# Expert feed-forward of a fused kernel: tokens fetched by indirect transfers, 18 weight slots, 12 of them loaded in the last projection

## The reference, cut to what matters

```
def expert_choice_ffn(xn, router_w, w_gate, w_up, w_down):
    b, n, d = xn.shape
    cap = CAPACITY_FACTOR * n // N_EXPERTS          # 64
    logits = jnp.einsum('bnd,de->ben', xn, router_w).astype(jnp.float32)
    aff = jax.nn.softmax(logits, axis=1)            # over the experts
    gate, idx = lax.top_k(aff, cap)
    xg = jax.vmap(lambda xs, ix: xs[ix])(xn, idx)
    hid = jax.nn.silu(jnp.einsum('becd,edf->becf', xg, w_gate)) * jnp.einsum('becd,edf->becf', xg, w_up)
    y = jnp.einsum('becf,efd->becd', hid, w_down) * gate[..., None].astype(xn.dtype)
    scatter = lambda ix, ys: jnp.zeros((n, d), ys.dtype).at[ix.reshape(-1)].add(ys.reshape(-1, d))
    return jax.vmap(scatter)(idx, y)
```

## Time and profile before

| | us |
|---|---|
| median of 3 executions | 3516.3 |
| lowest and highest | 3516.07, 3517.92 |
| span of the profiled execution | 3517.1 |
| TensorE busy in the span | 3333.0 (95%) |
| VectorE busy | 1738.0 |
| ScalarE busy | 673.3 |
| GpSimd busy | 302.6 |
| transfers: bytes, mean rate | 453.36 MB, 129 GB/s |
| expert part | from about 2972 to the end |

### The profile page before, as it was taken

The page is one execution under the profiler, slowest core; times in us unless marked ns, Lnnn a source line. Parts: engine busy times, 40 slices in busy tenths (PEclk is TensorE's granted clock), DMA queues, the critical chain, the costliest instruction groups (busy, mean ns, idle before and its releaser), DMA issues. The chain is left out here.

```text
span 3517.1 us, 39734 instructions
## 1 busy us (share of the span) xinstructions
PE 3333.0 (95%) x15231; PEld 2389.2 (68%) x15231; DVE 1738.0 (49%) x2533; ACT 673.3 (19%) x1097; POOL 302.6 (9%) x238
## 2 busy tenths in 40 slices
PE   6999998999999999999899999899989998899998
PEld 5888854488887888855478887555765887434342
DVE  4665457366646666348276644524336655211122
ACT  1111015111101111013221100531553101100001
POOL 2111000111100111000101100100330000000000
PEclk9999998999999999999899999999999999999999
DMA  5443221334322433222224321322113232899996
GB/s 134 117 104 102 80 60 36 84 90 117 95 82 84 115 94 101 91 56 60 70 74 114 94 90 48 92 72 84 43 30 90 84 108 100 355 409 409 410 410 267
DMA packets 469520, 453.36 MB, mean 129 GB/s; under 512 B 33867, under 2 KB 418174, under 8 KB 469149
## 3 DMA queue, kind: packets, MB, share of 16 engines
q1 hardware_dynamic: 467312, 449.97, 39.8%
q10 hardware_dynamic: 1452, 1.67, 0.4%
q0 software_dynamic: 640, 0.15, 0.0%
HBM read 445.96 MB, written 5.77 MB: 128 GB/s over the span
## 5 line engine op out<-in xcount | busy, mean ns | idle before, releaser
L465 PE MATMUL psum<-arena 128*128 128x256 f32 x7392 | 1616.2, 380 | 2.3 <-DVE arena L814 2.3
L465 PEld LDWEIGHTS psum<-arena 128*128 128x128 f32 x7392 | 1398.9, 190 | 203.9 <-issue 7.0
L879 DVE TENSOR_TENSOR arena<-arena 128x512 f32<-128x512 f32 (+2 forms) x152 | 96.4, 634 | 602.7 <-PE psum L465 573.6
L2360 PE MATMUL psum<-arena 128*64 128x512 f32 x1536 | 345.8, 600 | 1.6 <-ACT arena L2457 1.6
L354 POOL TENSOR_TENSOR arena<-arena 128x1024 f32<-128x1024 f32 x96 | 180.9, 1906 | 1037.6 <-DVE arena L869 993.0
L2360 PEld LDWEIGHTS psum<-arena 128*64 128x64 f32 x1536 | 104.8, 137 | 235.5 <-issue 228.4
L703 ACT COPY arena<-psum 128x256 f32<-128x256 f32 x104 | 38.9, 374 | 1177.1 <-PE psum L465 1177.0
L1677 PE MATMUL psum<-arena 128*128 128x256 f32 x1120 | 243.0, 379 | 1.4 <-DVE arena L2082 1.4
L1677 PEld LDWEIGHTS psum<-arena 128*128 128x128 f32 x1120 | 211.7, 189 | 32.6 <-DVE arena L2082 1.8
L575 PE MATMUL psum<-arena 128*128 128x512 f32 x416 | 183.1, 595 | 10.0 <-DVE arena L1021 6.3
L869 DVE TENSOR_REDUCE arena<-arena 128x256 f32<-128x2048 f32 x48 | 177.5, 3698 | 0.0
(11 more groups left out here) (422 smaller groups left out, 3011.9 us busy)
## 6 DMA issues: line engine op xcount, KB each, us to landing
arena<-in_w_gate_dram SPq DMA_DIRECT2D x64, 1024.0 KB, 14.0
arena<-in_w_up_dram SPq DMA_DIRECT2D x64, 1024.0 KB, 15.0
arena<-in_w_down_dram SPq DMA_DIRECT2D x64, 1024.0 KB, 17.4
arena<-in_ffn_w_gate_dram SPq DMA_DIRECT2D x88, 512.0 KB, 6.2
arena<-in_ffn_w_up_dram SPq DMA_DIRECT2D x88, 512.0 KB, 7.2
arena<-in_ffn_w_down_dram SPq DMA_DIRECT2D x96, 384.0 KB, 3.7
arena<-in_w_in_dram SPq DMA_DIRECT2D x144, 256.0 KB, 3.2
arena<-in_ada_w_dram SPq DMA_DIRECT2D x48, 512.0 KB, 4.0
```

The lines of the kernel that those rows point to most:

```text
L465: mm = pe.matmul(psum[:, b0 + b, c:c + HT], w, right(x), start=(first and c == 0), stop=last, skip_group_check=True)
L879: dve.tensor_tensor(sv[:, 0, :, :], a21, a22, ALU.add)
L2360: mm = pe.matmul(psum[64 * e:64 * e + 64, bank0 + half, :], x[:, k, 64 * e:64 * e + 64], ring[u % SLOTS][:, e, half * 512:(half + 1) * 512 ...
```

## The change

Weights: 18 slots instead of 12. Twelve of them lie in places of `arena` that the last projection no longer uses; their loads (0 to 11, the gate weights of pair 0 and four of up) are issued in the mixer, four each behind `joint_load` 16, 17 and 18. Six more follow in the head: 12 and 13 once the squares are used, 16 and 17 once the residual is transposed, 14 and 15 once the token rows are written out. Tokens: the normalised rows `xf_tok` are written to device memory (2 MB). For each pair, the two row matmuls (`rows_of`) now come first, VectorE computes for each of the 128 places its token's number (`tokens_of`), and GpSimd fetches the 128 rows of 4 KB by one indirect transfer; PE transposes them in eight matmuls (`gathered`) instead of multiplying with `one_hot`. Within a pair `put_back` lies after units 3, 5, 7 and 9, two before and two after the transposes; `rows_of(q + 1)` after unit 11, `gathered(q + 1)` after the fifth down unit. All loops are written out. The final norm's weight is loaded after the last expert load.

```diff
@@ second_mixer_program
+        dead = ((xm_at, xm_at + 2048), (xm_at + 24576, xm_at + 26624), (xm_at + 4096, xm_at + 6144),
+                (xm_at + 20480, xm_at + 22528), (xm_at + 12288, xm_at + 14336), (xm_at + 28672, xm_at + 30720))
+        mem["slots_from"] = xm_at
+        mem["expert_slots"] = [arena[:, at:at + 2048].rearrange("p (e c) -> p e c", e=2) for two in dead for at in two]
...
+            early = mem["expert_slots"]
             for u in range(16, 20):
                 joint_load(u, "w_o_2", (u - 16) * 256)
+                if u < 19:
+                    sp.wait_ge(unit_done, JOINT + u)
+                    for n in range(4 * (u - 16), 4 * (u - 16) + 4):
+                        name, k = ("w_gate_2", "w_up_2")[n // KT], n % KT
+                        src = d[name][0, 0:2, k * 128:(k + 1) * 128, :]
+                        sp.dma_start(early[n], src.rearrange("e p c -> p e c")).then_inc(mem["expert_in"][n], 16)
@@ experts_program, SyncE
+            sp.wait_ge(s["var_done"], 1)
+            load(12)
+            load(13)
+            sp.wait_ge(s["tok_ok"], 2 * NT)
+            load(16)
+            load(17)
+            for t in range(NT):
+                sp.wait_ge(s["xf_ok"], t + 1)
+                sp.dma_start(xf_dram[t * 128:(t + 1) * 128, :], xf_tok[:, t, :]).then_inc(s["xf_out"], 16)
+            sp.wait_ge(s["xf_out"], 16 * NT)
+            load(14)
+            load(15)
+            for n in range(SLOTS, UNITS * PAIRS):
+                sp.wait_ge(s["unit_used"], used(n - SLOTS))
+                load(n)
+            last = UNITS * PAIRS - SLOTS + (2 - UNITS * PAIRS) % SLOTS
+            sp.wait_ge(s["unit_used"], used(last))
+            sp.dma_start(final_w, d["final_norm_w_2"].partition_broadcast(128)).then_inc(s["final_in"], 16)
@@ GpSimd
+            pool.wait_ge(s["xf_out"], 16 * NT)
+            for q in range(PAIRS):
+                pool.wait_ge(s["token_ok"], q + 1)
+                if q:
+                    pool.wait_ge(s["xg_tr"], 2 * q)
+                pool.indirect_dma_start(xg_tok, None, xf_dram,
+                                        bass.IndirectOffsetOnAxis(ap=index[:, 0:1], axis=0))\
+                    .then_inc(s["gather_in"], 16)
@@ TensorE
+            def gathered(q):
+                pe.wait_ge(s["gather_in"], 16 * q + 16)
                 for k in range(KT):
-                    for t in range(NT):
-                        mm = pe.matmul(psum[:, 4 + k // 4, (k % 4) * 128:(k % 4 + 1) * 128],
-                                       xf_tok[:, t, k * 128:(k + 1) * 128],
-                                       one_hot[:, t, bass.ds(q * 128, 128)],
-                                       start=(t == 0), stop=(t == NT - 1))
+                    mm = pe.transpose(psum[:, 2 + k // 4, (k % 4) * 128:(k % 4 + 1) * 128],
+                                      xg_tok[:, k * 128:(k + 1) * 128], ident)
+                    if k % 4 == 3:
+                        mm.then_inc(s["xg_tr"], 1)
...
             for u in range(2 * KT):
+                    both_experts(2 * (u // KT), xg, UNITS * q + u, u % KT)
+                    if q and u in (3, 5, 7, 9):
+                        put_back_after(q - 1, (u - 3) // 2)
+                    if u == 11 and q + 1 < PAIRS:
+                        pe.wait_ge(s["silu_ok"], q + 1)
+                        rows_of(q + 1)
+                if q:
+                    for m in (4, 5):
+                        put_back_after(q - 1, m)
...
+                    both_experts(6, hidT, UNITS * q + 2 * KT + k, k)
+                    if k == 4 and q + 1 < PAIRS:
+                        gathered(q + 1)
@@ VectorE
+            dve.tensor_tensor_scan(token_iota, xg_tok[:, 0:T], xg_tok[:, 0:T], 0.0, ALU.mult, ALU.add)
...
+            def tokens_of(q):
+
+                sc = scatters[:, q % 3, :]
+                dve.wait_ge(s["rows_done"], q + 1)
+                dve.tensor_scalar(sc, psum[:, 0, :], slot_of_part, None, ALU.is_equal)
+                dve.drain()
+                dve.scalar_tensor_tensor(out=xg_tok[:, 0:T], in0=token_iota, scalar=1.0, in1=sc,
+                                         op0=ALU.mult, op1=ALU.mult, accum_out=token)
+                dve.drain()
+                dve.tensor_scalar(index[:, 0:1], token, -1.0, None, ALU.add)
+                dve.scalar_tensor_tensor(out=xg_tok[:, T:2 * T], in0=psum[:, 1, :], scalar=1.0, in1=sc,
+                                         op0=ALU.mult, op1=ALU.mult, accum_out=gates[:, q % 2:q % 2 + 1])
```

More of the change, by code:

```diff
@@ L2378, in pair @@
                 for u in range(2 * KT):
[L2379 to L2392, removed]
@@ L2403, in pair @@
[L2403 to L2408, removed]
-            pe.wait_ge(s["hot_ok"], 1)
-            pe.wait_ge(s["tok_ok"], 2 * NT + 2)
-            pe.wait_ge(s["xf_ok"], NT)
-            gather(0)
-            pair(0, 1, 1)
-            with pe.Fori(0, PAIRS - 2) as i:
-                pair(i + 1, 0, 1)
@@ L2417, in _ @@
-            pair(PAIRS - 1, 0, 0)
+                    if k % 4 == 3:
+                        mm.then_inc(s["hT_done"], 1)
+                if q:
+                    for m in (6, 7):
+                        put_back_after(q - 1, m)
+                for k in range(KT):
+                    if k == 0:
+                        pe.wait_ge(s["hT_act"], q + 1)
+                    if k == 4:
+                        pe.wait_ge(s["hT_dve"], q + 1)
+                    both_experts(6, hidT, UNITS * q + 2 * KT + k, k)
+                    if k == 4 and q + 1 < PAIRS:
+                        gathered(q + 1)
@@ L2418, in _ @@
+            pe.wait_ge(s["slot_ok"], 1)
+            pe.wait_ge(s["const_in"], 32)
+            rows_of(0)
+            gathered(0)
+            for q in range(PAIRS):
+                pair(q)
             for m in range(2 * NT):
                 if m >= 4:
-                    pe.wait_ge(s["res_ok"], KT * (PAIRS - 1) + m - 3)
+                    pe.wait_ge(s["res_ok"], 8 * (PAIRS - 1) + m - 3)
                 put_back(PAIRS - 1, m, m % 4)
@@ L2575, in _ @@
-            gathered()
             def add_back(q, m, bank):
@@ L2583, in weigh @@
             def weigh(q):
-                dve.wait_ge(s["unit_used"], q * 24 + (SLOTS + 3 * KT))
-                dve.scalar_tensor_tensor(out=y, in0=psum[:, 6:8, :].rearrange("p b c -> p (b c)"), scalar=gate,
-                                         in1=gate_row, op0=ALU.mult, op1=ALU.mult).then_inc(s["y_free"], 1)
-            def pair(q, first, more):
-                if not first:
+                dve.wait_ge(s["unit_used"], used(UNITS * q + UNITS - 1))
+                dve.scalar_tensor_tensor(out=y, in0=psum[:, 6:8, :].rearrange("p b c -> p (b c)"),
+                                         scalar=gates[:, q % 2:q % 2 + 1], in1=gate_row,
+                                         op0=ALU.mult, op1=ALU.mult).then_inc(s["y_free"], 1)
@@ L2591, in pair @@
+            def pair(q):
+                if q == 0:
+                    dve.wait_ge(s["tok_ok"], 2 * NT + 2)
+                else:
                     weigh(q - 1)
[L2592 removed]
+                    for m in range(4):
                         add_back(q - 1, m, 4 + m % 2)
+                if q + 1 < PAIRS:
+                    tokens_of(q + 1)
                 dve.wait_ge(s["silu_ok"], q + 1)
[L2595 to L2596 removed]
@@ L2607, in pair @@
-                dve.drain()
-                dve.sem_inc(s["scat_ok"], 1)
+                dve.wait_ge(s["unit_used"], used(UNITS * q + 2 * KT - 1))
+                for h in range(2):
+                    part = hid[:, h * 512:h * 512 + 512]
+                    dve.tensor_tensor(part, part, psum[:, 2 + h, :], ALU.mult).then_inc(s["hid_ok"], 1)
+                if q:
+                    for m in (4, 5):
+                        add_back(q - 1, m, 4 + m % 2)
+                dve.wait_ge(s["hT_done"], 2 * q + 2)
@@ L2617, in _ @@
             dve.memset(f_rstd, 1.0).then_inc(s["f_one"], 1)
-            pair(0, 1, 1)
-            with dve.Fori(0, PAIRS - 2) as i:
-                pair(i + 1, 0, 1)
-            pair(PAIRS - 1, 0, 0)
+            tokens_of(0)
+            gathered(0)
+            for q in range(PAIRS):
+                pair(q)
             weigh(PAIRS - 1)
+            dve.wait_ge(s["final_in"], 16)
             for t in range(NT):
```

208 lines of the change are left out of this document (94 added, 114 removed).

## The result

The changed kernel takes 3502.7 us (median of 4 executions, 3502.6 to 3503.2), the kernel before 3516.2 beside it: ratio 0.9958, 95% interval 0.9944 to 0.9973. That is 13.5 us less; 16.6 less, 3500 us, was forecast. Of the 15.6 us between the two profiled spans (3517.1 and 3501.5) 2.5 lie ahead of any change: the first load of the last projection is issued at 2891.8 in the one and at 2889.3 in the other, and the expert part begins at 2971.9 and 2969.4. From there to the end it takes 545.2 us before and 532.1 after, 13.1 less. I use this length, "the expert part", beside the medians, since it begins between 2964.7 and 2971.8 in the traces of kernels that are alike up to that point.

A forecast was written before the change was run, and what follows sets the result against it. PE set the pace, 1% below the transfer ceiling; afterwards the weight stream would. Restart 3024.0 + 174 x 2.571 + gathers 9.0 = 3480.4, plus unit 1.9 and tail 18.2: 3500.5, -16.6 us, taken off the median: 3500 us; eight-in-ten range 3487 to 3512.

The forecast's parts named there:

- work taken off PE alone gives almost nothing: Expert stage: PE's weight demand (406 GB/s) is 1% below the transfer ceiling (409), so lighter PE gains almost nothing per pair.
- 45 us taken off PE: Expert pairs: the 45 us taken off PE are worth nothing beyond the point where PE starts waiting for weights.
- Part 1: Early loads and 18 slots: 174 loads instead of 180 after the stream's restart, -15.4 us.
- Early loads hidden: Last projection: its loads 17 to 19 line up behind expert weights, yet the cost is 0 us.
- already hidden: Early loads: six of the twelve replace loads already hidden ahead of the restart, so only six count as gain.
- Part 2: Indirect gather for matmuls: PE's pair falls from 62.0 to 54.8 us; seven gathers cost the stream 1.28 us each, +9.0.
- Part 3: Head, top-k to first unit: first unit 3.4 us later, stream restart at 3024.0, 5.0 us later.
- The sum: Stream end 3480.4, one unit after it 1.9, tail 18.2: end 3500.5 against 3517.1, -16.6 us, hence 3500 us.
- unit 125: Expert stage: where PE catches up with the weight stream, in pair 5, and waits for weights from there on.
- the line 3 + 2.28n: Expert stage: time in us after the first unit's start at which PE reaches unit n; landing is 5 + 2.62(n - 17).
- about 61 us per pair early: Expected sign in the windows: about 61 us per pair early, falling to 55 where PE leads, near 63 where it waits.
- The clock rival: PE's clock falls in waits for weights from pair 5 on: +3 to +6 us, 3505; chance 0.09.

The follow-up runs named there:

- e2: Changed kernel with 12 slots instead of 18: early loads stay in the last projection, the six loads of the head go; 3518.3 us.
- e3: Changed kernel with PE's eight gather transposes of pairs 1 to 7 done four times over instead of once; 3501.9 us.
- e5: Changed kernel with PE's eight gather transposes of pairs 1 to 7 done ten times over, a pair of 62.0 us as before the change; 3515.3 us.
- e6: Changed kernel with no expert load in the last projection: the first twelve are issued in the experts' head; 3506.9 us.
- e1: Changed kernel with only pair 0's rows fetched, the indirect transfers of pairs 1 to 7 left out, engines doing the same work; 3493.7 us.
- e8: Changed kernel with each fetch of pairs 1 to 7 issued a second time when the first has landed; 3512.0 us.
- e12: e11 with PE kept busy in the head by 49 matmuls before the row matmuls and 30 during the fetch; 3497.1 us, 0.9944 of the kernel before.
- e10: e9 with PE kept busy by 49 matmuls while VectorE picks the tokens and 26 while the first rows are fetched; 3502.2 us.
- e11: e9's split head, with loads 14 and 15 issued when pair 0's rows have landed instead of when token rows are written out; 3501.1 us.
- e7: Changed kernel with idle PE filled in the head: 32 matmuls while VectorE picks the tokens, 30 while the first rows are fetched; 3501.5 us.
- e9: Changed kernel, pair 0's head split: VectorE starts after the first row matmul, GpSimd is told the tokens before the gate sum; 3502.7 us.

## Why the prediction was right

- *Which bound holds.* That after the change the stream sets the end is shown by e2 and e3, and that fewer loads alone are worth nothing while PE's pair is 62.0 us by e5. That work taken off PE alone gives almost nothing holds per pair, as the prediction has it; at the end of the stage it gave 14.1 us, and e2 comes out at nothing because fetches and head cost as much. The prediction's sum has this right. Its "45 us taken off PE" has no working: 62.0 - 54.8 over seven pairs is 50.
- *Part 1, 174 loads for 180.* -15.4 forecast, 15.6 by e2's median, 15.0 by its trace. Early loads hidden: PE is busy as before in the projection (12.00 us of 12 in three windows, 10.64 in the fourth, where it was 10.63), and its last weight sums and the last issue of its loads lie as long before the expert part as they did. That the first twelve were "already hidden" is shown by e6 to within 4 us.
- *Part 2, the fetches.* +9.0 forecast, 9.0 (e1) and 9.3 (e8) by the medians.
- *Part 3, the head.* Restart against the beginning of the expert part: 47.1 us before, 52.3 after, +5.2; +5.0 forecast. That these agree is partly luck. The fetch landed in 4.7 us where I had put 7.2, 2.5 too much. Against it stand 0.9 that GpSimd began after VectorE's last operation, which I had left out, 0.5 between the first unit's start and the restart, and 1.3 of the 1.5 us by which the stretch ahead of the places took longer; I had allowed 0.2. This last is not the change's doing: in e2, e3, e5 and e8, with the same code there, the clock rose earlier and the stretch took 30.3 to 30.4 us, as before. In e2 the restart came 3.0 us later than before, not 5.2. The two row matmuls took 3.8 us at half clock; my 3.6 was short of twice 1.9.
- *The sum.* Stream end to last expert matmul 1.9 forecast, 2.8 measured (the last expert weights land at 3481.3, 0.8 behind the end reckoned from the share; the last unit takes 2.0). The stream's 458.8 us are 1.1 above 174 x 2.571 + 9.0 + 1.3 for the final weight. Its transfer was issued before the last expert weights had landed and ran among them; I had not counted it into the stream's end. In the window from 3025 the stream ran at share 0.85, which is 0.8 of the 1.1. A PE at half clock is not the cause: in e12, at full clock throughout, the share dips in the same way (0.89 over five us). Why it dips stays open. The tail is 18.2 us, as forecast.
- *Side numbers that failed.* I let PE meet the stream near unit 125, in pair 5, and ascribed it 30 us of slack. Its first wait for a weight comes at 3193, at unit 81 in pair 3, and the slack is 44 us. In the line 3 + 2.28n I had left out pair 0's missing put-backs (8.5 us), which I had subtracted in the total, and the pair took 54.0 us, not 54.8; with both put right the two lines meet near unit 92, and the slower start of the stream brings that to 87. The sign "about 61 us per pair early" failed too and contradicts my own 54.8: the pairs took 54.0 from the first on. The end did not hang on these.
- *The clock rival.* From 3193 on PE has gaps of 0.6 us in many units, and the granted clock stayed 1.00 over all 400 us. In the head, where PE idled 11.7 us, it had fallen to 0.50. The Trainium skill ("TensorE: Matmul & The Clock Gate", HAM oscillation) describes a kernel whose waits for transfers, several us long, let the clock fall at every tile. The head's idle time agrees with that; the waits of 0.6 us are much shorter than the ones it describes, and the clock stayed up through them. A short gap is not safe by itself, though: in e10 PE idled 0.72 us before the row matmuls, was busy from there on, and the clock was 0.94 from 3003 to 3006 and 0.50 from 3006 to 3009.
- *What the forecast missed.* It had the change at -16.6 us; the medians give -13.5, the expert parts -13.1. The 3.5 us between the forecast and the traces are all found: 0.2 in the head, 2.4 in the stream (1.3 for the final weight, 1.1 more), 0.9 behind its end.

## What to carry to other kernels

Where two resources run within a per cent of each other, work out when each one's path would end alone, since an edit that shortens one is worth no more than the distance to the other, here 15 us from PE's path to the stream's. Price what the edit adds to the other path, and test the halves apart. When a transfer stream is the bound, price every edit by bytes, by how many loads stand ready when it restarts, and by the moment when its first slot comes free; read slack from the periods of the two, not from the waits listed. Look for idle PE time just ahead of the step that restarts the stream, and for transfers that the one urgent fetch must pass.

## What the runs showed of the hardware that I had not expected

- An indirect fetch of 128 rows of 4 KB keeps GpSimd 0.94 to 1.05 us. It landed after 4.4 to 4.7 us with no other transfer at its side (e2, e11, e12), 4.2 to 4.7 with two loads issued 5 to 7 us before it (e1, e3 to e5, e8, the changed kernel; 5.5 in e7), 6.3 and 7.0 with them issued 3 us before it (e9, e10), and 7.6 in the median under the full stream, 8.2 at most. The weights landed 18.6 us after theirs. So it did not queue behind them:

```profile
arena<-in_w_gate_dram SPq DMA_DIRECT2D x64, 1024.0 KB, 18.6
...
arena<-gathered_from,expert_tokens POOLq DMA_INDIRECT x8, 7.6
```

- Eighteen slots did not put more than some seven loads in line. A load landed 18.6 us after its issue, seven times the 2.57 us that one takes. SyncE's issue of a load took 0.4 us in the head and 2.36 in the full stream, near the time of one load:

```profile
L2298 SPq DMA_DIRECT2D arena<-in_w_gate_dram x8: 470/2358/5350, 3214.3 to 3232.3; - x8
```

- PE at half clock did a pair of row matmuls in 3.8 us for 2.0 (e12), and unit 0 freed its slot 3.7 us after its start for 2.0. With 1.28 us idle between filling and transposes (e10) the clock was 0.65 from 3015 to 3018 and 0.50 in unit 0; with none (e7, e12) it stayed 1.00.
- The moment when the clock rises at the beginning of the expert part differs between executions of the same code, from about 4 to about 7 us after it, and with it 1.2 to 1.5 us of the head's length.
